# Gathering an expert's two vectors as two transfers instead of one, in a one-core transformer kernel

## The chip, the cores and the metric

The kernel runs on one core of a Trainium2 chip (trn2). The metric is the device time of one execution in microseconds (us), as a median of several runs. A difference of about 0.2% (4.6 us) is the least that counts here.

## What is computed

Two transformer blocks over 256 tokens of width 2048. The first block has a mixer (gated linear attention beside dilated attention) and then a mixture of very many small experts; the second has three mixers, cross attention to a memory of 256 rows, and a last norm. The change lies in the expert part of the first block, which is:

```python
def peer_ffn(xn, w_query, sub_keys, expert_down, expert_up):
    ...
    top_s, top_i = lax.top_k(sc, PEER_TOPK)
    ...
    best_s, best_pos = lax.top_k(cand_s, PEER_TOPK)
    idx = jnp.take_along_axis(cand_i, best_pos, axis=-1)
    gates = jax.nn.softmax(best_s, axis=-1)
    K = PEER_HEADS * PEER_TOPK

    def block(args):
        xb, ib, gb = args
        u = expert_down[ib]
        act = jax.nn.gelu(jnp.einsum('tkd,td->tk', u, xb).astype(f32))
        vv = expert_up[ib]
        return jnp.einsum('tk,tkd->td', (gb * act).astype(vv.dtype), vv)
```

There are 16,384 experts. Each has a down vector and an up vector of 2048 float32 (8 KB each). Each token has 8 heads, and each head picks 16 experts, so each token takes 128 experts: it multiplies its own normed row with the down vector, puts the result through gelu, weighs it with the gate, and adds that multiple of the up vector to its output.

## The kernel before

The kernel is written for the engines one by one, with semaphores. The function `peer` holds the expert stage. The tokens stand in two tiles of 128, one token in each partition. A unit is one head of one tile, 16 units in all (`UNITS`), with 16 experts each (`K`); the counter `d = n * K + j` runs over 256 steps, and a step is one expert for each of 128 tokens.

`slots` is a ring of four slots (`DEPTH = 4`). A slot has two halves of 8 KB in each partition: half 0 for the down vector, half 1 for the up vector. The array `peer_rows` in memory has an expert's down and up vector side by side, 16 KB a row (made in `lay_out`). What each engine does in a step:

- POOL waits until the unit's row numbers are written (`selected`), and until the add of four steps earlier is over (`added`), and then issues one indirect DMA (L1635): 128 rows of 16 KB, 2 MB. It counts up `row_in` of the slot when landed.
- DVE waits for `row_in` and multiplies half 0 with the normed tokens, summed to one number a token (`dotted`, L1727; in the trace CUSTOM_DVE_ANT_0 and the READ_ACCUMULATOR behind it). Text and headings here call this the dot.
- ACT waits for the dot, computes gelu, multiplies with the gate, waits for the add two steps earlier, and scales the identity with the result (L1569, L1570, L1573; `diag_ready`).
- PE waits for `diag_ready` and multiplies this diagonal matrix with half 1 in four matmuls of 512 columns (L1495), which add up in four PSUM banks over a whole tile. This is the add; it counts up `added`. PE has no wait for the gather of its own, since the dot of the same slot lies behind the same landing.

Beside these steps, in the same order of each engine's code: for the first six units PE computes the query of unit n + 2, two of its matmuls a step (L1464), ahead of that step's add; DVE selects the experts of unit n + 1 in pieces ahead of the dots of steps 1 to 6 (`SELECT_AT`), the last of which writes `rows`, the row numbers of the gathers; ACT and DVE compute the gates at steps 8 and 10 (`GATE_AT`). In units 7 to 13 the memory of the second block is loaded (SP), normed, transposed and multiplied with its key and value weights. Ahead of the dot of step 1 of unit 8, DVE waits for the last add of the first tile and adds the four banks to the residual (`take_sums`, L1700), and PE's first add of the second tile waits for that. After the last add the same is done for the second tile, and only then does the second block begin.

SP loads the query weights and the memory's weights in transfers of 1 MB with rows of 8 KB (`load_query`, L1380), on the hardware queue q1. The gathers run on the software queue q0.

The row numbers have two buffers, by the unit's parity.

Of the kernel before, what the change touches and what calls it, by code (L numbers as in the profile page):

```python
# [1382 lines left out]
def peer(k, query_in, keys_in, gain_in, rstd, name="peer"):  # L1383
    nc, ins, B = k.nc, k.ins, k.banks
    UNITS, K, DEPTH = NT * PEER_H, PEER_TOP, 4
# [11 lines left out]
    slots = shaped(k.ring[:, :], DEPTH, 2, D)  # L1397
# [12 lines left out]
    rows = area.take(2, K).bitcast(U32)  # L1410
# [14 lines left out]
    S = lambda n: k.sem(f"{name}_{n}")  # L1425
    query_done, query_out, scored, stored, staged_done = S("query_done"), S("query_out"), S("scored"), S("stored"), S("staged")
    first_query, first_out, first_scored, first_staged = (S(n) for n in ("first_query", "first_out", "first_scored", "first_staged"))
    selected, gated, gates_ready, own, act_own = (S(n) for n in ("selected", "gated", "gates_ready", "own", "act_own"))
    dotted, added, diag_ready, acc_out, gained = (S(n) for n in ("dotted", "added", "diag_ready", "acc_out", "gained"))
    mem_in, mem_squared, mem_meaned, mem_rooted, mem_own, mem_scaled, mem_turned, mem_out = (S(n) for n in (  # L1430
        "mem_in", "mem_squared", "mem_meaned", "mem_rooted", "mem_own", "mem_scaled", "mem_turned", "mem_out"))
    row_in = [S(f"row_in{i}") for i in range(DEPTH)]

    with nc.Block() as block:
        @block.sync
# [13 lines left out]
        def _(pe):  # L1449
# [38 lines left out]
            def add_row(n, j):  # L1488
                d = n * K + j
                first, last = n % PEER_H == 0 and j == 0, n % PEER_H == PEER_H - 1 and j == K - 1  # L1490
                if first and n:
                    pe.wait_ge(acc_out, 4)
                pe.wait_ge(diag_ready, d + 1)
                for c in range(4):
                    m = pe.matmul(B[c][:, :], diag[:, d % 2, :], slots[:, d % DEPTH, 1, c * 512:(c + 1) * 512], start=first, stop=last)  # L1495
                m.then_inc(added, 1)
# [128 lines left out]

        @block.gpsimd
        def _(pool):
            for n in range(UNITS):
                pool.wait_ge(selected, n + 1)
                for j in range(K):  # L1630
                    d = n * K + j
                    if d >= DEPTH:
                        pool.wait_ge(added, d - DEPTH + 1)
                    pool.nop(nofuse=True)
                    pool.indirect_dma_start(slots[:, d % DEPTH, :, :].rearrange("p a b -> p (a b)"), None, ins["peer_rows"],  # L1635
                                            bass.IndirectOffsetOnAxis(ap=rows[:, n % 2, j:j + 1], axis=0)) \
                        .then_inc(row_in[d % DEPTH], 16)

        @block.vector
        def _(dve):  # L1640
# [19 lines left out]
            def select(n, p):  # L1660
                for c in range(2):
                    if n == 0 and c == 0:
                        dve.wait_ge(first_staged, 1)
                    else:
                        dve.wait_ge(staged_done, n + 1)
                    top16(staged[:, p, c, :], top[:, p, c, :], top_i[:, c, :], rest[:, c, :])
                    yield
                dve.tensor_copy(top_f[:, :, :], top_i[:, :, :])
                step(dve.tensor_tensor(cand[:, 0, :, :], top[:, p, 0, :].unsqueeze(2).to_broadcast([P, K, K]),
                                       top[:, p, 1, :].unsqueeze(1).to_broadcast([P, K, K]), ALU.add))  # L1670
                yield
                top16(flat(cand[:, 0, :, :]), best[:, p, :], best_i, flat(cand[:, 1, :, :]))
                yield
                dve.tensor_scalar(low[:, p, :], best[:, p, 0:1], -1.0, None, ALU.mult)
                dve.tensor_scalar(part_i[:, 0, :], best_i, 4, None, ALU.logical_shift_right)
                step(dve.tensor_scalar(part_i[:, 1, :], best_i, 15, None, ALU.bitwise_and))
                step(dve.tensor_copy(part_f[:, :, :], part_i[:, :, :]))
                for c in range(2):
                    m = dve.tensor_tensor(hot[:, c, :, :], part_f[:, c, :].unsqueeze(2).to_broadcast([P, K, K]),
                                          k.c("iota").unsqueeze(1).to_broadcast([P, K, K]), ALU.is_equal)  # L1680
                step(m)
                yield
                for c in range(2):
                    m = dve.tensor_tensor(hot[:, c, :, :], hot[:, c, :, :], top_f[:, c, :].unsqueeze(1).to_broadcast([P, K, K]),
                                          ALU.mult)
                step(m)
                step(dve.tensor_reduce(pair[:, :, :], hot[:, :, :, :], AX.X, ALU.add))
                dve.scalar_tensor_tensor(rows[:, p, :], pair[:, 0, :], float(PEER_K), pair[:, 1, :], ALU.mult, ALU.add) \
                   .then_inc(selected, 1)

# [14 lines left out]
            for n in range(UNITS):  # L1705
                p, t = n % 2, n // PEER_H
                pieces = select(n + 1, 1 - p) if n + 1 < UNITS else iter(())
                for j in range(K):
# [14 lines left out]
                            dve.tensor_scalar(mem[:, m, :], mem[:, m, :], mem_ms[:, m:m + 1], None, ALU.mult).then_inc(mem_scaled, 1)  # L1723
                    d = n * K + j
                    row = slots[:, d % DEPTH, 0, :]
                    dve.wait_ge(row_in[d % DEPTH], 16 * (d // DEPTH + 1))
                    dve.tensor_tensor_reduce(row, row, xn[:, t, :], 1.0, 0.0, ALU.mult, ALU.add, dots[:, p, j:j + 1]) \  # L1727
                       .then_inc(dotted, 1)
            take_sums(1)
# [1181 lines left out]
def lay_out(i):  # L2911
    a = {}
# [40 lines left out]
    a["w_query"] = blocks_of(i["peer_w_query"][0], 2 * PEER_K)  # L2953
    a["sub_keys"] = np.ascontiguousarray(i["peer_sub_keys"][0].transpose(3, 0, 1, 2).reshape(P, 2 * PEER_H, PEER_K))
    a["norm2_row"] = rows(i["norm2_g"])
    a["peer_rows"] = np.concatenate([i["peer_down"][0], i["peer_up"][0]], axis=1)
    parts = {}
    for n, v in (("norm1_g", "norm1_g"), ("norm2_g", "norm2_g"), ("mix_g", "mix_norm_g_2"), ("xa_g", "xa_norm_g_2"),
                 ("mem_g", "mem_norm_g_2")):
# [18 lines left out]
```

## Time and profile before

| | us |
|---|---|
| runs (3): median, lowest, highest | 2311.83, 2311.35, 2314.30 |
| profiled execution, its own time | 2310.28 |
| profiled execution, span from first to last instruction | 2308.5 |
| PE busy | 2056.2 (89%) |
| DVE busy | 1293.5 (56%) |
| ACT busy | 810.2 (35%) |
| POOL busy | 266.9 (12%) |
| software queue q0 (gathers): 36864 packets, 536.89 MB | 54.8% of 16 engines' span |
| hardware queue q1 (all other loads and stores): 53232 packets, 191.63 MB | 25.9% |
| first gather to last add | 470.6 to 1792.0 |

The busy time of an engine is an average over very different parts of the kernel. In the expert stage the DMA engines are the ones to look at: the profile gives for any stretch the mean busy share of the 16 DMA engines and the bytes that they moved. Times of waits are idle time of an engine just before an instruction, put down to what released it. The TensorE clock in the expert stage was granted in full but for short drops (mean 0.98 from 480 to 1784 us).

### The profile page before, as it was taken

The numbers are of one execution on the slowest core, as the hardware profiler recorded it, in microseconds if no ns is written. First come the engines' busy times: TensorE is split into PE (matmuls) and PEld (weight loads), VectorE is DVE, ScalarE is ACT, GpSimd is POOL, SyncE is SP. The second block draws the span as 40 slices with busy tenths as digits, with TensorE's granted clock in tenths as the row PEclk, the third lists the DMA queues.
The fourth block names the chain that finished last, engine by engine and source line by source line (L and its number), as shares of the span: only waits on it lengthen the run. The fifth ranks groups of instructions, "written<-read, shape, count | busy, mean of one in ns | idle before, by whom it ended". The sixth has DMA issues, their size and how long they took to land. (4 is left out here: it accounts for less than half of the span.)

```text
span 2308.5 us, 21761 instructions
## 1 busy us (share of the span) xinstructions
PE 2056.2 (89%) x8141; PEld 1333.0 (58%) x8141; DVE 1293.5 (56%) x2008; ACT 810.2 (35%) x1743; POOL 266.9 (12%) x267
## 2 busy tenths in 40 slices
PE   7999999989988989977777898899877799999997
PEld 6878778854444444422223344444322798999886
DVE  5545655455555556545566555555644766475555
ACT  6445564312222222212222222122122555355453
POOL 0000000011122112122121111211211000000000
PEclk9999999999999999989999999999999899999999
DMA  6545566499999999999999999999998656466662
GB/s 231 165 133 160 163 191 202 185 376 428 428 426 427 428 427 424 428 427 415 428 412 428 428 428 426 427 424 428 409 429 380 210 155 181 125 204 203 183 194 80
DMA packets 90201, 729.90 MB, mean 316 GB/s; under 512 B 10448, under 2 KB 10704, under 8 KB 53104
## 3 DMA queue, kind: packets, MB, share of 16 engines
q0 software_dynamic: 36864, 536.89, 54.8%
q1 hardware_dynamic: 53232, 191.63, 25.9%
q8 instruction: 64, 1.05, 0.2%
q14 instruction: 41, 0.34, 0.0%
HBM read 724.28 MB, written 4.19 MB: 316 GB/s over the span
## 5 line engine op out<-in xcount | busy, mean ns | idle before, releaser
L1495 PE MATMUL bank<-ring,work 128*128 128x512 f32 x2048 | 964.4, 615 | 199.0 <-ACT work L1573 196.2
L1727 DVE CUSTOM_DVE_ANT_0 ring<-ring,mix_t 128x2048 f32<-128x2048 f32 x256 | 586.8, 2292 | 555.4 <-DMA ring<-in_peer_rows_dram,work 553.4
L1495 PEld LDWEIGHTS bank<-ring,work 128*128 128x128 f32 x2048 | 375.6, 193 | 712.5 <-issue 379.2
L490 DVE TENSOR_TENSOR ring_r<-ring,ring_r 128x1024 fp32r<-128x1024 f32 (+2 forms) x300 | 334.5, 1144 | 306.0 <-ACT ring_r L469 305.4
L1635 POOL DMA_INDIRECT ring<-in_peer_rows_dram,work x256 | 262.9, 1027 | 1508.7 <-PE bank L1495 952.9
L523 PE MATMUL bank<-ring_r,mix_r 128*128 128x512 f32 (+1 forms) x1312 | 400.8, 392 | 0.0
L1569 ACT ACTIVATE work<-work 128x1 f32<-128x1 f32 x256 | 51.9, 203 | 959.0 <-DVE work L1727 958.9
L469 ACT ACTIVATE ring_r<-ring 128x1024 fp32r<-128x1024 f32 (+2 forms) x300 | 288.5, 992 | 166.3 <-DMA ring<-in_w_out_dram 50.5
L523 PEld LDWEIGHTS bank<-ring_r,mix_r 128*128 128x128 f32 x1312 | 244.6, 189 | 47.0 <-issue 1.0
L523 PE MATMUL bank<-ring_r,act_r 128*128 128x512 f32 (+1 forms) x608 | 234.6, 386 | 0.0
L520 PE MATMUL bank<-mix_r,ring_r 128*128 128x256 f32 (+1 forms) x1216 | 225.9, 288 | 5.6 <-DVE ring_r L490 5.6
L520 PEld LDWEIGHTS bank<-mix_r,ring_r 128*128 128x128 f32 (+1 forms) x1216 | 190.6, 191 | 7.4 <-DVE ring_r L490 4.1
L520 PE MATMUL bank<-act_r,ring_r 128*128 128x256 f32 (+1 forms) x608 | 173.1, 285 | 0.0
L1464 PEld LDWEIGHTS bank<-act_t,h 128*128 128x128 f32 x544 | 102.9, 190 | 62.8 <-issue 55.0
L1464 PE MATMUL bank<-act_t,h 128*128 128x256 f32 x544 | 137.2, 379 | 0.0
L523 PEld LDWEIGHTS bank<-ring_r,act_r 128*128 128x128 f32 x608 | 114.7, 189 | 22.2
L520 PEld LDWEIGHTS bank<-act_r,ring_r 128*128 128x128 f32 (+1 forms) x608 | 116.1, 191 | 0.0
L1573 ACT ACTIVATE work<-const,work 128x128 f32<-128x128 f32 x256 | 102.8, 401 | 8.4
L523 PE MATMUL bank<-ring_r,h_r 128*128 128x512 f32 x288 | 83.2, 394 | 0.9 <-DVE h_r L2788 0.9
L1570 ACT ACTIVATE work<-work 128x1 f32<-128x1 f32 x256 | 75.3, 294 | 8.3
L523 PEld LDWEIGHTS bank<-ring_r,h_r 128*128 128x128 f32 x288 | 53.8, 188 | 12.7 <-DVE h_r L2788 1.3
L523 PE MATMUL bank<-ring_r,work_r 128*128 128x512 f32 x192 | 59.8, 392 | 0.0
(397 smaller groups left out, 1233.4 us busy)
## 6 DMA issues: line engine op xcount, KB each, us to landing
ring<-in_w_in_dil_dram SPq DMA_DIRECT2D x72, 512.0 KB, 3.6
ring<-in_w_out_dram SPq DMA_DIRECT2D x64, 512.0 KB, 3.6
ring<-in_w_in_mo_dram SPq DMA_DIRECT2D x48, 384.0 KB, 3.4
h<-in_w_query_dram SPq DMA_DIRECT2D x15, 1024.0 KB, 11.4
ring<-in_w_in_gla_dram SPq DMA_DIRECT2D x24, 512.0 KB, 3.6
ring<-in_w_in_ml_oz_dram SPq DMA_DIRECT2D x24, 512.0 KB, 3.7
h<-in_xa_wkv_dram SPq DMA_DIRECT2D x8, 1024.0 KB, 22.4
ring<-in_w_in_lru_dram SPq DMA_DIRECT2D x16, 512.0 KB, 3.6
```

The lines of the kernel that those rows point to most:

```text
L469: act.activation(high(c), raw(c), ACT.Copy).then_inc(k.weights_high, 1)
L490: dve.tensor_tensor(low(c), raw(c), plain(high(c)), ALU.subtract).then_inc(k.weights_low, 1)
L520: m = pe.matmul(bank[0:job.m, 0:T], w[:, q, g * job.m:(g + 1) * job.m], a[:, q, :], start=start, stop=stop)
L523: m = pe.matmul(bank[:, 0:job.cols], a[:, q, g * P:(g + 1) * P], w[:, q, :], start=start, stop=stop)
L1464: m = pe.matmul(bank[:, f * T:(f + 1) * T], a, w, start=kc == 0, stop=kc == KC - 1)
L1495: m = pe.matmul(B[c][:, :], diag[:, d % 2, :], slots[:, d % DEPTH, 1, c * 512:(c + 1) * 512], start=first, stop=last)
L1569: step(act.activation(gelu[:, p, j:j + 1], dots[:, p, j:j + 1], ACT.Gelu_apprx_tanh))
L1570: step(act.activation(coef[:, p, j:j + 1], gelu[:, p, j:j + 1], ACT.Copy, scale=gates[:, p, j:j + 1]))
L1573: act.activation(diag[:, d % 2, :], k.c("ident"), ACT.Copy, scale=coef[:, p, j:j + 1]).then_inc(diag_ready, 1)
L1635: pool.indirect_dma_start(slots[:, d % DEPTH, :, :].rearrange("p a b -> p (a b)"), None, ins["peer_rows"], bass.IndirectOffsetOnAxis(ap=ro ...
L1727: dve.tensor_tensor_reduce(row, row, xn[:, t, :], 1.0, 0.0, ALU.mult, ALU.add, dots[:, p, j:j + 1]) \
```

## The change

The two vectors of an expert come from two arrays, `peer_down` and `peer_up`, with 8 KB a row, and by two indirect DMAs of 1 MB each. Each of them has its own semaphores, `down_in` and `up_in`. POOL asks for the down vectors of step d as soon as the dot of step d - 4 is over (`dotted`), and behind that for the up vectors of step d - 1 as soon as the add of step d - 5 is over (`added`). So the order on the queue is down 0, down 1, up 0, down 2, up 1, and so on. DVE's dot waits for `down_in`. PE's add waits for `up_in` as well, behind `diag_ready`. Since row numbers are now read one step later, DVE waits ahead of writing the row numbers of unit n for the last add of unit n - 2.

```diff
-    row_in = [S(f"row_in{i}") for i in range(DEPTH)]
+    down_in = [S(f"down_in{i}") for i in range(DEPTH)]
+    up_in = [S(f"up_in{i}") for i in range(DEPTH)]
...
                 pe.wait_ge(diag_ready, d + 1)
+                pe.wait_ge(up_in[d % DEPTH], 16 * (d // DEPTH + 1))
...
         @block.gpsimd
         def _(pool):
-            for n in range(UNITS):
-                pool.wait_ge(selected, n + 1)
-                for j in range(K):
-                    d = n * K + j
-                    if d >= DEPTH:
-                        pool.wait_ge(added, d - DEPTH + 1)
-                    pool.nop(nofuse=True)
-                    pool.indirect_dma_start(slots[:, d % DEPTH, :, :].rearrange("p a b -> p (a b)"), None, ins["peer_rows"],
-                                            bass.IndirectOffsetOnAxis(ap=rows[:, n % 2, j:j + 1], axis=0)) \
-                        .then_inc(row_in[d % DEPTH], 16)
+            def gather(d, half, source, landed):
+                n, j = divmod(d, K)
+                pool.nop(nofuse=True)
+                pool.indirect_dma_start(slots[:, d % DEPTH, half, :], None, source,
+                                        bass.IndirectOffsetOnAxis(ap=rows[:, n % 2, j:j + 1], axis=0)).then_inc(landed[d % DEPTH], 16)
+
+            def gather_up(d):
+                if d >= DEPTH:
+                    pool.wait_ge(added, d - DEPTH + 1)
+                gather(d, 1, ins["peer_up"], up_in)
+
+            for d in range(UNITS * K):
+                if d % K == 0:
+                    pool.wait_ge(selected, d // K + 1)
+                if d >= DEPTH:
+                    pool.wait_ge(dotted, d - DEPTH + 1)
+                gather(d, 0, ins["peer_down"], down_in)
+                if d:
+                    gather_up(d - 1)
+            gather_up(UNITS * K - 1)
...
+                if n >= 2:
+
+                    dve.wait_ge(added, (n - 1) * K)
                 dve.scalar_tensor_tensor(rows[:, p, :], pair[:, 0, :], float(PEER_K), pair[:, 1, :], ALU.mult, ALU.add) \
                    .then_inc(selected, 1)
...
-                    dve.wait_ge(row_in[d % DEPTH], 16 * (d // DEPTH + 1))
+                    dve.wait_ge(down_in[d % DEPTH], 16 * (d // DEPTH + 1))
...
-    a["peer_rows"] = np.concatenate([i["peer_down"][0], i["peer_up"][0]], axis=1)
+    a["peer_down"], a["peer_up"] = i["peer_down"][0], i["peer_up"][0]
```

## Rows read from the trace of the kernel before

**Rows 1.** The page's slices: 40 of 57.7 us; DMA share in tenths, then GB/s.

```profile
DMA  6545566499999999999999999999998656466662
GB/s 231 165 133 160 163 191 202 185 376 428 428 426 427 428 427 424 428 427 415 428 412 428 428 428 426 427 424 428 409 429 380 210 155 181 125 204 203 183 194 80
```

**Rows 2.** Waits, 480 to 1750: us in total, times, the longest.

```profile
POOL ring L1635 <- PE bank L1495: 932.7, 224, 20.2
...
DVE ring L1727 <- DMA ring<-in_peer_rows_dram,work: 532.7, 226, 5.1
```

**Rows 3.** Stretches: length, busy us (instructions) by engine, PE clock, DMA share, GB/s.

```profile
500.00:505.00 5.00, 5.00 (x15) 2.50 (x15) 4.58 (x11) 0.90 (x3) 3.56 (x2) 1.00 0.85 311
1060.00:1070.00 10.00, 7.40 (x16) 2.88 (x16) 5.38 (x9) 2.29 (x8) 3.54 (x3) 1.00 0.87 346
1155.00:1175.00 20.00, 16.21 (x35) 6.11 (x34) 14.61 (x33) 6.37 (x15) 6.62 (x4) 0.98 0.93 382
1610.00:1630.00 20.00, 18.25 (x49) 8.79 (x50) 9.20 (x8) 3.81 (x13) 5.58 (x5) 1.00 0.94 387
...
1690.00:1780.00 90.00, 68.05 (x148) 26.60 (x149) 41.40 (x36) 16.17 (x54) 16.38 (x18) 1.00 1.01 428
480.00:1784.00 1304.00, 1105.39 (x2768) 505.85 (x2767) 720.47 (x1090) 301.94 (x885) 258.97 (x252) 0.98 1.00 424
```

**Rows 4.** DMA queues, 1100 to 1150: packets, MB, their time over 16 engines' stretch.

```profile
q0 software_dynamic: 1477, 21.35, 100.4%
```

**Rows 5.** DMA queues, 459 to 462: loads with rows of 8 KB alone.

```profile
DMA packets 174, 1.29 MB, mean 431 GB/s; under 512 B 16, under 2 KB 16, under 8 KB 16
...
q1 hardware_dynamic: 174, 1.29, 102.1%
```

**Rows 6.** DMA queues, 730 to 745: gathers beside loads with rows of 8 KB.

```profile
q0 software_dynamic: 312, 4.51, 71.0%
q1 hardware_dynamic: 256, 1.84, 29.3%
```

**Rows 7.** The gathers' line, L1635: the last row of its view.

```profile
DMA to landing us min/median/max: 8.8/11.7/25.0
```

**Rows 8.** Timeline near the stage's end: start, us, engine, line, what, idle before.

```profile
1760.44 2.29 DVE L1727 CUSTOM_DVE_ANT_0 ring<-ring,mix_t 128x2048 f32<-128x2048 f32 x1 [2.61 <-DMA ring<-in_peer_rows_dram,work]
...
1763.79 3.70 PE L1495 MATMUL bank<-ring,work 128*128 128x512 f32 x8 [1.20 <-ACT work L1573]
1765.34 2.29 DVE L1727 CUSTOM_DVE_ANT_0 ring<-ring,mix_t 128x2048 f32<-128x2048 f32 x1 [2.60 <-DMA ring<-in_peer_rows_dram,work]
...
1768.27 0.94 POOL L1635 DMA_INDIRECT ring<-in_peer_rows_dram,work  x1 [3.97 <-PE bank L1495]
...
1784.90 2.29 DVE L1727 CUSTOM_DVE_ANT_0 ring<-ring,mix_t 128x2048 f32<-128x2048 f32 x1 [2.58 <-DMA ring<-in_peer_rows_dram,work]
...
1788.26 3.70 PE L1495 MATMUL bank<-ring,work 128*128 128x512 f32 x8 [1.18 <-ACT work L1573]
```

**Rows 9.** Timeline, 1055 to 1065: an add and the gather that waits for it.

```profile
1055.53 3.70 PE L1495 MATMUL bank<-ring,work 128*128 128x512 f32 x8 [1.20 <-ACT work L1573]
...
1062.69 2.40 POOL L1635 DMA_INDIRECT ring<-in_peer_rows_dram,work  x1 [6.65 <-issue]
```

**Rows 10.** Timeline at the boundary of the two tiles.

```profile
1148.79 2.48 DVE L1700 TENSOR_TENSOR x_res<-bank,x_res 128x512 f32<-128x512 f32 x4
...
1153.08 2.29 DVE L1727 CUSTOM_DVE_ANT_0 ring<-ring,mix_t 128x2048 f32<-128x2048 f32 x1
...
1157.49 2.82 POOL L1635 DMA_INDIRECT ring<-in_peer_rows_dram,work  x1 [7.05 <-PE bank L1495]
```

**Rows 11.** Timeline at the stage's start: the first dot and the fifth gather.

```profile
483.97 2.28 DVE L1727 CUSTOM_DVE_ANT_0 ring<-ring,mix_t 128x2048 f32<-128x2048 f32 x1
...
495.61 0.93 POOL L1635 DMA_INDIRECT ring<-in_peer_rows_dram,work  x1 [20.20 <-PE bank L1495]
```

**Rows 12.** Timeline: the query matmuls of one step.

```profile
507.56 1.03 PE L1464 MATMUL bank<-act_t,h 128*128 128x256 f32 x4
```

## What is expected, worked out before the changed kernel was run

> **What bounds the kernel now.** I read the page's slices first, then the waits, then the stage in stretches, then single DMA queues, then the timeline. The slices show a stage of some 1300 us (slices 9 to 31 of 57.7 us) in which the DMA engines stand at 9 tenths and carry 409 to 429 GB/s in all but the first and the last slice [rows 1]. That is the expert stage: 256 gathers of 2 MB, 536.9 MB of the 729.9 MB of the whole kernel. The waits of that stretch say the same from the engines' side: DVE stands 532.7 us for the gathered rows, and POOL stands 932.7 us for PE to give a slot back [rows 2]. POOL's number is the larger one, but it is no bottleneck as long as transfers asked for earlier still keep the DMA engines busy. So the question for each edit is what it does to the bytes per microsecond, not what it does to a wait.
>
> The stretches answer how full the DMA is [rows 3]: 428 GB/s at share 1.01 where nothing disturbs (1690 to 1780 us), 424 GB/s over the stage from 480 to 1784 us. At 428 GB/s a gather of 2,097,152 bytes takes 4.90 us, which is the distance of two dots in the timeline (1760.44 to 1765.34) [rows 8]. The missing part is 1304 x (1 - 424/428) = 12.2 us. Four stretches hold most of it: 5 x (1 - 311/428) = 1.4, 10 x (1 - 346/428) = 1.9, 20 x (1 - 382/428) = 2.1, 20 x (1 - 387/428) = 1.9, together 7.4 us, and in these the DMA share is below 1: the engines have run dry. The other 4.8 us lie spread in stretches with a full share and I count them as not to be had.
>
> **Why it runs dry.** Four slots of 2 MB. A slot is asked for again when its add is over: from the start of dot 1760.44 the add runs 1763.79 to 1767.49 and POOL starts the new gather at 1768.27, 7.8 us after the data came [rows 8]. The landing takes 11.7 us in the median, 8.8 at the least [rows 7]; 7.8 + 11.7 = 19.5 is four times 4.9. An undisturbed gather could come 11.7 - 8.8 = 2.9 us sooner than it does, so 2.9 us is about how late POOL may be before the engines go empty. It is later in the four stretches: at 1062.69 the gather starts 3.5 us after PE ended its add (1055.53 + 3.70) and takes 2.40 instead of 0.94 [rows 9]; after the first tile's sums (DVE 2.48 us, which PE waits for) POOL starts at 1157.49 after 7.05 us idle and takes 2.82 [rows 10]; at the start the fifth gather goes out only at 495.61, 11.6 us after the first dot starts [rows 11].
>
> **The change part by part.**
>
> Depth of the queue (gain). The down half of a slot is now free after its dot, and the up half after its add; 8 transfers of 1 MB (2.45 us each) stand in the place of 4 of 2 MB. When a down vector lands, seven others of 1 MB are asked for or on their way: 7 x 2.45 = 17.1 us. Its half is asked for again after the dot (2.29) and POOL's step, about 3.3 us: 13.8 us in hand. For an up half: add 3.70 and POOL's 0.8, 4.5 us, 12.6 us in hand. The same count for before is 3 x 4.90 - 7.8 = 6.9. So the tighter of the two gains 12.6 - 6.9 = 5.7 us on top of the 2.9 us, 8.6 us. The stops above are 3 to 5 us and are covered. At the start the fifth down vector can go out at the end of the first dot (486.3) and not at 495.61. I count the whole of the 7.4 us as gained. The bounds are 0 (the stops stay) and 12.2 us (all of the shortfall).
>
> The boundary of the tiles is the place that becomes harder. DVE, ahead of the second dot of the second tile, waits for the last add of the first, and now dots run ahead of adds: an up vector lands 7.3 us (three transfers) after its down vector. With T the landing of down vector 128, up vector 127 lands at T + 2.45, its add ends at T + 6.2, the sums (2.48) at T + 8.7, and with the piece of expert selection behind them (1151.27 to the dot at 1153.08, 1.8 us) [rows 10] dot 129 starts at T + 10.5 and not at T + 4.9. Behind it on POOL stand down vector 133 and all that follows, 5.6 us late. That is inside the 8.6 us, though not by much; I cost it at nothing, and at some 2 us if the cover is smaller.
>
> The end (gain). Before, the chain behind the last byte is dot 1784.90, ACT, add 1788.26 to 1791.96: 7.1 us [rows 8]. Now the order of landing is down 255, up 254, up 255. If the last byte comes at the same 1784.90, up 254 is there at 1782.45, its add ends at 1786.15, and the last add ends at 1786.15 + 3.70 = 1789.85. That is 2.1 us less; the last dot and its ACT steps lie under the two up vectors.
>
> Rows of 8 KB for rows of 16 KB (cost). The bytes stay the same, the packets of the gathers double: 128 rows of 8 KB and 16 small packets in each of 512 transfers. What a 16 KB packet takes: 1477 packets of 21.35 MB are 1303 rows, 1.004 x 50 us x 16 engines = 803 us, 0.6164 us each with its share of the small ones [rows 4]. What an 8 KB packet takes is not shown for a gather, but for the 1 MB loads of the query weights. Alone on the engines: 1.29 MB are 158 rows, 1.021 x 3 us x 16 = 49.0 us, 0.3102 us each, at 431 GB/s in that short stretch [rows 5]. Beside gathers: 1.84 MB are 225 rows, 0.293 x 15 x 16 = 70.3 us, 0.3125 us each, where a 16 KB packet of the same stretch takes 0.710 x 240 / 275 = 0.6196 [rows 6]. Two halves against one whole, times the 8 rows that an engine has of a gather and 256 gathers (2048): (0.6204 - 0.6164) x 2048 = 8.2 us from the stretch with one queue, (0.6250 - 0.6196) x 2048 = 11.1 us from the mixed one, and 0 if one reads the 431 GB/s. The worst pair of these numbers, 0.6250 against 0.6164, gives 17.6 us, and one more small packet for each engine and gather (some 9 ns by difference of these rows, an estimate) 20 us. I take 8.2, since there, as in the expert stage, one queue has the engines nearly to itself.
>
> POOL. 512 gathers in place of 256. Each costs 0.94 us, and at most the 0.8 us from an add's end to POOL's start (1767.49 to 1768.27) [rows 8] for what stands between two, so at most 3.4 us of each 4.9. A long one (2.82) [rows 10] makes that 5.3 once, which the 8.6 us in hand cover. POOL stays faster than the DMA. POOL works in order: down vector d waits for dot d - 4, and behind it up vector d - 1 for add d - 5. That add ends 3.7 us after its up vector's landing, 1.1 us before dot d - 3 ends, for which the next command waits, so in the steady state neither holds up the other.
>
> PE's wait for the up vector, and DVE's wait for earlier adds. PE's wait stands ahead of the four matmuls of an add, behind the query matmuls of that step; these run while the vector is on its way. Queued behind it is the next step's query. PE has 3.70 busy of 4.90, with a query step of 1.03 [rows 12] it is 4.73: still under. DVE's added wait, ahead of the write of the gather's row numbers, is for adds of a whole unit (16 experts, 78 us) earlier and costs nothing.
>
> **The sum.** The profiled execution: 2310.3 us, of which the span is 2308.5; 2310.3 - 7.4 - 2.1 + 8.2 = 2309.0. The median of the runs is 2311.8, 1.5 above the profiled one, so the forecast is 2310.5.
>
> **The rivals.**
> 1. Small packets cost nothing. For it: the 431 GB/s of the stretch with 8 KB rows alone. Against it: in both stretches two 8 KB packets last longer than one of 16 KB. The time: 2311.8 - 7.4 - 2.1 = 2302.3, and 2297.5 if the whole 12.2 us come back. Chance 0.27 for this side.
> 2. Small packets cost more than the deeper queue gives. The place is each DMA engine, 4096 more rows of its own; the price is 17.6 to 20 us, and the time 2311.8 - 9.5 + 20 = 2322.3, slower. It decides from (9.5 + 4.6) / 2048 = 7 ns for each 16 KB on. For it: the 0.3125 us beside gathers, and that a gather's rows are scattered while the weights' are not. Against it: the 4 to 5 ns that like-for-like rows give. Chance 0.21.
> 3. The queue gets no deeper in effect, since POOL works in order and a late add holds back down vectors too. The stops stay, the cost of the rows is paid: 2311.8 - 2.1 + 8.2 = 2317.9. Against it: the 1.1 us above and 8.6 us in hand. Chance 0.05.
> 4. A transfer's own fixed time. Each transfer would be paid for with a part that does not overlap. The trace: landing takes 11.7 us and yet one gather is done each 4.90 us [rows 7, 8], so such a part is under other transfers, and 1 MB loads alone reached 431 GB/s [rows 5]. If 1 MB ran at 80% of the rate of 428, the stage's 537 MB would take 314 us more, 2626. Chance 0.01. The Trainium skill, "DMA: Bandwidth & Descriptors", section "Bandwidth", gives 341 GB/s for a transfer of 1 MB and 425 for 16 MB, and asks for 1 MiB or more; by its two figures the change would be much slower, and by that rule the trace disagrees, since its figures are for transfers one by one.
>
> **How the numbers follow.** The forecast's own case (within 4.6 us, 0.2%, about the least that a measurement of this kernel tells from no change) has 0.46, from 2307 to 2316. Faster by over 0.2%: 0.27. Within: 0.46. Slower: 0.27, from rivals 2, 3 and 4. The range holds rival 1 down to 2300 and rival 2 up to 2325; the bare bounds, 2297.5 and 2331.8 (cost 20 and no gain), lie outside with what is left.
>
> **What the profile after would show.** Gathers: 512, and 73,728 packets on the software queue. If the queue's depth is right, the four stretches have a DMA share of 1 and no slice of the stage under 425 GB/s but for the ends. If the price of the rows is right, two dots are 4.93 us apart in the undisturbed part (4.90 for rival 1, 4.97 for rival 2), and the mean of an 8 KB packet is 0.310 us. DVE's waits for rows should shrink little, since the bytes bound it; PE should now wait for the DMA (up vectors) instead of ACT. Landing should become longer (some 17 us), which is no loss. The last add should end 5 us behind the last dot's place in time. The prediction is wrong if the gathers' rate falls below 424 GB/s in undisturbed stretches, or if new dry stretches appear at the tiles' boundary.

## The result and the profile after

| | before | after |
|---|---|---|
| runs: median, lowest, highest (us) | 2311.59, 2310.40, 2314.30 (4 runs) | 2326.27, 2325.08, 2327.23 (4 runs) |
| profiled execution, its own time and span (us) | 2310.28, 2308.5 | 2327.14, 2325.4 |
| software queue q0: packets, MB | 36864, 536.89 | 73728, 536.90 |
| POOL busy (us) | 266.9 | 547.1 |

The ratio is 1.0062, with a 95% interval of 1.0044 to 1.0079: 14.7 us slower by the medians. The forecast was 2310.5 with a range of 2300 to 2325, so the result lies 1.3 us above it, on the side of rival 2.

The page of the changed kernel: its slices of 58.1 us, the gathers' queue, and the costliest groups of the stage (busy us, mean ns of one, idle before and what ended it).

```profile
DMA  6545566499999999999999999999998656466662
GB/s 230 163 136 161 159 194 208 175 391 421 421 421 421 421 421 422 421 421 421 422 421 421 421 422 421 422 421 419 422 421 370 203 146 186 124 204 200 186 194 80
...
q0 software_dynamic: 73728, 536.90, 55.5%
...
L1497 PE MATMUL bank<-ring,work 128*128 128x512 f32 x2048 | 955.2, 610 | 223.3 <-DMA ring<-in_peer_up_dram,work 197.6
...
L1633 POOL DMA_INDIRECT ring<-in_peer_up_dram,work x256 | 286.8, 1120 | 637.4 <-PE bank L1497 618.6
```

Against [rows 1] two things have changed. The dips (415, 412, 409) are gone: the stage's rate is level. And the level is 421 and not 428. PE now waits for the up vectors, as intended. The same stretches as in [rows 3], of the changed kernel (length, busy us and instructions of PE, PEld, DVE, ACT, POOL, PE clock, DMA share, GB/s):

```profile
500.00:505.00 5.00, 5.00 (x17) 2.88 (x17) 4.13 (x11) 1.30 (x4) 3.36 (x3) 1.00 1.01 421
1060.00:1070.00 10.00, 7.38 (x17) 2.88 (x16) 4.60 (x4) 2.10 (x7) 3.96 (x4) 1.00 1.01 419
1155.00:1175.00 20.00, 16.31 (x33) 6.36 (x33) 16.78 (x37) 2.70 (x9) 9.99 (x8) 0.91 1.01 417
1610.00:1630.00 20.00, 18.31 (x49) 8.79 (x48) 9.20 (x8) 3.60 (x12) 7.93 (x9) 1.00 1.01 420
1690.00:1780.00 90.00, 66.59 (x146) 26.06 (x145) 41.40 (x36) 16.58 (x55) 35.72 (x37) 1.00 1.01 421
480.00:1784.00 1304.00, 1083.91 (x2745) 501.63 (x2743) 716.66 (x1086) 300.20 (x877) 534.67 (x504) 0.98 1.01 421
```

The four dry stretches (shares 0.85 to 0.94 before) all stand at 1.01. So the queue does not run dry there any more, and what is lost is lost all along the stage. The timeline of the changed kernel shows it in the dots, and what follows the last of them (start, us, engine, line, what, idle before):

```profile
1741.82 2.29 DVE L1742 CUSTOM_DVE_ANT_0 ring<-ring,mix_t 128x2048 f32<-128x2048 f32 x1 [2.67 <-DMA ring<-in_peer_down_dram,work]
...
1786.54 2.29 DVE L1742 CUSTOM_DVE_ANT_0 ring<-ring,mix_t 128x2048 f32<-128x2048 f32 x1 [2.67 <-DMA ring<-in_peer_down_dram,work]
...
1796.43 2.29 DVE L1742 CUSTOM_DVE_ANT_0 ring<-ring,mix_t 128x2048 f32<-128x2048 f32 x1 [2.63 <-DMA ring<-in_peer_down_dram,work]
...
1799.00 7.10 PE L1497 MATMUL bank<-ring,work 128*128 128x512 f32 x16 [1.25 <-DMA ring<-in_peer_up_dram,work]
1806.14 2.48 DVE L1715 TENSOR_TENSOR x_res<-bank,x_res 128x512 f32<-128x512 f32 x4 [7.41 <-PE bank L1497]
```

Between the first two rows lie nine experts: 44.72 / 9 = 4.969 us each. The same count of before gives (1784.90 - 1760.44) / 5 = 4.892 [rows 8]. The difference is 0.077 us an expert, and times 256 it is 19.7 us. The first gather starts at 471.2 (470.6 before), and the last dot at 1796.43 (1784.90 before): 11.5 us later, 11.0 without the later start. The sums follow at 1806.14; before, they followed the end of the last add at 1791.96 [rows 8] at once. That is 14.2 us later. The span is 16.9 us longer; the other 2.7 us lie behind the stage, in these two executions, and the medians of the runs, 14.7 us apart, do not call for them.

### The profile page after: what moved, and what is told of

It reads as the page before. It is cut to its first block and busy times, and to the rows that moved or that the text cites. A ratio compares the mean times of both kernels' runs of the same rounds, so it can differ in the third digit from the quotient of the medians.

```text
span 2325.4 us, 22538 instructions
## 1 busy us (share of the span) xinstructions
PE 2047.4 (88%) x8141; PEld 1334.4 (57%) x8141; DVE 1294.8 (56%) x2008; ACT 811.5 (35%) x1743; POOL 547.1 (24%) x523
## 3 DMA queue, kind: packets, MB, share of 16 engines
q0 software_dynamic: 73728, 536.90, 55.5%
## 5 line engine op out<-in xcount | busy, mean ns | idle before, releaser
L1633 POOL DMA_INDIRECT ring<-in_peer_up_dram,work x256 | 286.8, 1120 | 637.4 <-PE bank L1497 618.6
L1633 POOL DMA_INDIRECT ring<-in_peer_down_dram,work x256 | 256.3, 1001 | 606.6 <-DVE work L1703 468.6
```

Of the source, the lines that this page charges most:

```text
L1633: pool.indirect_dma_start(slots[:, d % DEPTH, half, :], None, source, bass.IndirectOffsetOnAxis(ap=rows[:, n % 2, j:j + 1], axis=0)).then_ ...
```

## The experiments

The kernel before was run beside each, and the ratios are against it. Its medians lie between 2311.3 and 2312.8.

**Is it the two arrays, or the size of a row?** The changed kernel, reading both halves from the old array with 16 KB a row, in 8 KB pieces:

```diff
+            both = ins["peer_rows"].rearrange("n (a b) -> (n a) b", a=2)
...
-                pool.indirect_dma_start(slots[:, d % DEPTH, half, :], None, source,
-                                        bass.IndirectOffsetOnAxis(ap=rows[:, n % 2, j:j + 1], axis=0)).then_inc(landed[d % DEPTH], 16)
+                pool.indirect_dma_start(slots[:, d % DEPTH, half, :], None, both,
+                                        bass.IndirectOffsetOnAxis(ap=rows[:, n % 2, j:j + 1], axis=0), half * D).then_inc(landed[d % DEPTH], 16)
...
+                step(dve.tensor_scalar(pair[:, :, :], pair[:, :, :], 2.0, None, ALU.mult))
```

> The changed kernel, but both transfers read halves of 8 KB out of the one array of before (its rows of 16 KB lie side by side; row numbers doubled, up vectors at an offset of half a row). Theory 'rows': what costs is that an engine moves 16 rows of 8 KB for an expert in place of 8 of 16 KB. Then two dots stay 4.97 us apart in the undisturbed stretch and the time stays at that of the changed kernel, 2326 us (within 2). Rival 'two arrays': what costs is that the vectors lie in two arrays. Then the distance goes back to 4.90 us and the time to 2302 to 2308, since the dry stretches are gone.

Measured: 2325.61 us, ratio 1.0066 (1.0050 to 1.0083). Its dots are 4.98 us apart:

```profile
1746.79 2.29 DVE L1745 CUSTOM_DVE_ANT_0 ring<-ring,mix_t 128x2048 f32<-128x2048 f32 x1 [2.67 <-DMA ring<-in_peer_rows_dram,work]
1751.77 2.29 DVE L1745 CUSTOM_DVE_ANT_0 ring<-ring,mix_t 128x2048 f32<-128x2048 f32 x1 [2.68 <-DMA ring<-in_peer_rows_dram,work]
```

So where the halves lie in memory makes no difference that can be seen. The loss comes with asking for them in two pieces.

**Does the price grow with the number of pieces?** The changed kernel with the up vector split once more, in two arrays of 4 KB a row:

```diff
-                gather(d, 1, ins["peer_up"], up_in)
+                gather(d, 1, ins["peer_up_0"], up_in, 0)
+                gather(d, 1, ins["peer_up_1"], up2_in, 1)
```

> The changed kernel with the up vector in two arrays of half vectors, so three transfers for an expert: one of 128 rows of 8 KB, two of 128 rows of 4 KB. An engine now has 24 rows and 3 small packets for an expert; 8 and 1 before, 16 and 2 in the changed kernel. Theory 'rows': the same step once more, 0.077 us for an expert: dots 5.05 us apart, 2326 + 20 = 2346 us. Rival 'order': the loss of the change comes from the order of the two transfers and the waits behind it, which stay: 4.97 us and 2326. If POOL's commands were what bounds, three of them (3 x 1.24 = 3.7 us and the long ones) would give dry stretches with a DMA share under 1.

Measured: 2342.39 us, ratio 1.0139 (1.0122 to 1.0156), another 16 us where theory 'rows' had 20. In the timeline the dots are 5.04 us apart, and the slices have fallen to 415, two of them to 404 and 408:

```profile
GB/s 229 162 139 161 162 196 217 156 411 415 415 415 416 415 416 413 416 416 415 416 404 408 414 415 416 416 415 416 415 416 415 207 147 192 124 198 203 183 197 81
...
q0 software_dynamic: 110592, 536.92, 56.5%
...
1747.83 2.29 DVE L1746 CUSTOM_DVE_ANT_0 ring<-ring,mix_t 128x2048 f32<-128x2048 f32 x1 [2.75 <-DMA ring<-in_peer_down_dram,work]
1752.87 2.29 DVE L1746 CUSTOM_DVE_ANT_0 ring<-ring,mix_t 128x2048 f32<-128x2048 f32 x1 [2.74 <-DMA ring<-in_peer_down_dram,work]
```

An engine moves for each expert 8 rows and a small packet (before), 16 and 2 (after), 24 and 3 (here). The steps are 0.077 and 5.04 - 4.97 = 0.07 us, for 8 more rows and one more small packet each time: 9 to 10 ns for each row more, its part of the small packet included, whether rows of 16 KB are halved or rows of 8 KB. Row and small packet came together in every kernel, so these runs do not divide the price between them.

**Is the new order worth anything?** The changed transfers, with the old asking: both halves behind the add, down d and then up d.

```diff
-                    pool.wait_ge(dotted, d - DEPTH + 1)
+                    pool.wait_ge(added, d - DEPTH + 1)
                 gather(d, 0, ins["peer_down"], down_in)
-                if d:
-                    gather_up(d - 1)
-            gather_up(UNITS * K - 1)
+                gather(d, 1, ins["peer_up"], up_in)
```

> The changed kernel's two transfers and four slots, but both halves asked for behind the add, in the order down d, up d. The run with three slots and this order took 2395 us, more than any count had given, since the count left out what a landing needs beside its moving: 6.9 us at the least for 1 MB, 4.4 more than the 2.5 of moving. In hand then: three slots 9.9 - 5.7 - 4.4 = -0.2, four slots 14.9 - 5.7 - 4.4 = 4.8 us. Theory 'rows' (with the corrected count): no loss beside the changed kernel, distance 4.97 us, 2326 us within 3. Rival 'the new order is worth something by itself, and late asking is what costs': some 20 us or more above, 2345.

Measured: 2325.17 us, ratio 1.0058 (1.0042 to 1.0074), the same as the changed kernel. The dots are 4.97 us apart, and one slice of the stage dips to 405. So neither the order nor the early asking is worth anything that can be seen here, and the cost of the pieces is most of what the change does to the time.

**What would a deeper queue be worth without smaller rows?** The kernel before with a fifth slot. Its memory is that of the residual, so this kernel adds the sums to the normed tokens and computes another function.

```diff
-    UNITS, K, DEPTH = NT * PEER_H, PEER_TOP, 4
+    UNITS, K, DEPTH = NT * PEER_H, PEER_TOP, 5
...
-    slots = shaped(k.ring[:, :], DEPTH, 2, D)
+    ring4 = shaped(k.ring[:, :], 4, 2, D)
+    slot = lambda d: ring4[:, d % DEPTH, :, :] if d % DEPTH < 4 else k.x3
```

> The kernel before (one transfer of 2 MB with rows of 16 KB) with five slots in place of four. The fifth lies where the residual x stood, so the residual is not kept: the expert sums are added to the normed tokens instead, and tile 0 is copied over at the stage's end beside the last sums. That gives depth alone, without small rows. In hand: 4 x 4.90 - 7.8 - 3.9 (the least landing 8.8 less 4.9 of moving) = 7.9 us, against 3.0 with four slots. Theory 'depth gives the dry stretches back': distance 4.90 us, no slice of the stage under 425 GB/s, 2312 - 7.4 = 2304 to 2306 us. Rival 'slowest engine': the mean rate rises, but one of the 16 DMA engines has more to do and sets the landing of each gather; the time stays at 2309 to 2312 and the stage ends with a tail in which the DMA share is 0.1 or less.

Measured: 2310.03 us (11 runs), ratio 0.9989 (0.9979 to 0.9998). Its slices, two dots, the sums, and the last microseconds of the gathers:

```profile
GB/s 232 164 130 163 164 185 207 181 387 428 427 427 428 428 428 427 428 425 428 429 427 429 428 427 428 428 425 416 429 428 338 214 152 180 125 204 203 183 194 80
...
1752.53 2.29 DVE L1730 CUSTOM_DVE_ANT_0 x_res<-x_res,mix_t 128x2048 f32<-128x2048 f32 x1 [2.60 <-DMA x_res<-in_peer_rows_dram,work]
1757.42 2.29 DVE L1730 CUSTOM_DVE_ANT_0 ring<-ring,mix_t 128x2048 f32<-128x2048 f32 x1 [2.59 <-DMA ring<-in_peer_rows_dram,work]
...
1788.93 2.48 DVE L1703 TENSOR_TENSOR x_res<-bank,mix_t 128x512 f32<-128x512 f32 x4 [4.79 <-PE bank L1496]
...
1774.00:1776.00 2.00, 0.80 (x3) 0.31 (x3) 0.41 (x2) 0.90 (x3) 0.00 (x0) 1.00 0.81 344
1776.00:1778.00 2.00, 2.00 (x6) 0.94 (x5) 1.00 (x1) 0.00 (x0) 0.00 (x0) 1.00 0.15 66
1778.00:1780.00 2.00, 1.16 (x3) 0.19 (x1) 1.29 (x2) 0.61 (x3) 0.00 (x0) 1.00 0.06 25
1780.00:1782.00 2.00, 1.66 (x4) 0.87 (x5) 0.16 (x1) 0.29 (x1) 0.00 (x0) 1.00 0.04 16
```

The dips are gone but for one slice (416), and the kernel gains only 3.0 us at the sums (1791.96 to 1788.93) and 2.5 us by the ratio, where the prediction put 7.4 on the dips. The last four rows say why: most of the engines have moved all their data by 1776, and then a share of 0.06, one engine of sixteen, moves on at 25 GB/s until about 1781.4. A gather counts as landed when its last engine is done, so the mean rate is not what sets the dots; the engine that is last is.

The dots of the kernel before say the same. These are the two on either side of the third and of the fourth dry stretch of [rows 3]:

```profile
1161.34 2.29 DVE L1727 CUSTOM_DVE_ANT_0 ring<-ring,mix_t 128x2048 f32<-128x2048 f32 x1 [1.41 <-DMA ring<-in_peer_rows_dram,work]
1168.00 2.29 DVE L1727 CUSTOM_DVE_ANT_0 ring<-ring,mix_t 128x2048 f32<-128x2048 f32 x1 [1.90 <-DMA ring<-in_peer_rows_dram,work]
...
1621.16 2.29 DVE L1727 CUSTOM_DVE_ANT_0 ring<-ring,mix_t 128x2048 f32<-128x2048 f32 x1 [2.57 <-DMA ring<-in_peer_rows_dram,work]
1626.49 2.29 DVE L1727 CUSTOM_DVE_ANT_0 ring<-ring,mix_t 128x2048 f32<-128x2048 f32 x1 [3.04 <-DMA ring<-in_peer_rows_dram,work]
```

The four stretches lengthened one distance of two dots each: to 5.52 us (the dot at 510.04), 5.48 (1072.30), 6.66 and 5.33, together 3.4 us more than four times 4.89. With five slots the same four distances are 4.88, 5.01, 4.89 and 4.89. So these stretches held back the dots by about 3 us, and not by the 7.4 us that the mean rate had lost. The trace also keeps the landing of each of the sixteen parts of a gather. In the last stretch the first part of one gather came 7.5 us behind the first part of the one before it, and the last part 5.3 us behind the last: the engine that was ahead lost 2.6 us, and the one that was last 0.4 us.

The Trainium skill, "DMA: Bandwidth & Descriptors", section "Why a DMA increments its semaphore by 16 and not by 1", says that the up to 16 engines of a transfer finish independently and that only the full count means that all data landed. The trace agrees: the last dot, at 1781.84, comes when the single engine stops.

**Do dry stretches cost anything at all?** The changed kernel with three slots in place of four.

```diff
-    UNITS, K, DEPTH = NT * PEER_H, PEER_TOP, 4
+    UNITS, K, DEPTH = NT * PEER_H, PEER_TOP, 3
```

> The changed kernel with three slots in place of four. By the count of the prediction the tighter half has 5 x 2.49 - 4.5 = 7.9 us in hand, near the 6.9 of the kernel before, against 12.6 with four. Theory 'depth gave back what the dry stretches cost': some of the dry stretches come back, 2326 + 3 to 8, so 2329 to 2334. Rival 'slowest engine': the end of the gathers is set by those of the 16 DMA engines that lag (in the changed kernel a small part of them works some 6 us longer than the rest at the stage's end), and a deeper queue only lets the others run ahead. Then fewer slots cost nothing: 2324 to 2327, and the tail at the end is shorter.

Measured: 2327.67 us, ratio 1.0078 (1.0061 to 1.0094); the intervals of this and of the changed kernel overlap. Its slices and the end of its gathers, beside the end of those of the changed kernel:

```profile
GB/s 230 163 136 162 160 195 208 173 392 415 419 421 421 421 421 411 422 421 422 422 407 421 419 422 421 422 421 419 422 421 410 202 150 184 125 204 200 186 194 80
...
1796.00:1800.00 4.00, 2.76 (x8) 1.00 (x7) 2.30 (x2) 0.34 (x2) 0.00 (x0) 1.00 0.88 326
1800.00:1804.00 4.00, 4.00 (x10) 1.83 (x11) 0.00 (x0) 2.04 (x4) 0.00 (x0) 1.00 0.03 14
```

```profile
1792.00:1796.00 4.00, 2.73 (x7) 0.99 (x6) 1.80 (x2) 0.90 (x3) 0.00 (x0) 1.00 0.74 309
1796.00:1800.00 4.00, 2.75 (x8) 1.00 (x7) 2.30 (x2) 1.15 (x4) 0.00 (x0) 1.00 0.10 43
1800.00:1804.00 4.00, 4.00 (x11) 1.83 (x10) 0.00 (x0) 1.23 (x2) 0.00 (x0) 1.00 0.01 4
```

Dry stretches have come back (415, 411, 407) and the time has not moved. Most of the engines finish some 4 us later than with four slots (share 0.88 in place of 0.10 from 1796 to 1800), and the last one finishes within 1 us of where it did (its last part lands at 1802.2, and at 1801.3 with four slots). A dry stretch takes time mostly from engines that were ahead.

**How much reserve is there at each depth?** Two kernels, the changed one with three slots and the old asking, and the kernel before with three slots. The edits are those already shown.

> Three slots as in the run with depth 3, and both halves of a slot are asked for together, behind the add of the step that used it, as before the change (down d, then up d). In hand: 2 x 4.97 - 4.5 = 5.4 us, less than the 6.9 of the kernel before. Undisturbed distance of dots 4.97 by 'rows'. Theory 'depth': more dry time than the kernel before had (7.4 us in the four stretches), so 2326 + 9 to 15: 2335 to 2341. Rival 'slowest engine': 2326 to 2330. This is also the changed kernel without its new order, so if the order itself were at fault, the distance would fall under 4.97.

> The kernel before with three slots of 2 MB. In hand by the corrected count: 2 x 4.90 - 7.8 - 3.9 = -1.9 us, so the landing time and not the rate of the DMA engines would bound it: a slot turns once in 7.8 + 8.8 = 16.6 us, dots 5.5 us apart, 256 x 0.63 = 160 us more, 2470 us. If the count is wrong and only the rate matters: 2312 to 2330 us.

Measured: 2395.0 us, ratio 1.0376 (1.0324 to 1.0428), and 2593.81 us, ratio 1.1218 (1.1197 to 1.1239, two runs of it). A count of one slot's turn says where the loss begins. A slot is asked for again 7.8 us after its data came [rows 8], and the shortest landing follows, 8.8 us for 2 MB [rows 7]. This turn, at least 16.6 us, has to fit into as many periods as there are slots. Before: 4 x 4.89 = 19.6, 3 us to spare. Before with three slots: 14.7, too little. Changed, three slots, old asking, with its own shortest landing: 7.8 + 6.8 = 14.6 against 3 x 4.97 = 14.9, nothing to spare. The last rows of the landing view of the kernel before with three slots, and of the changed one with three slots and the old asking:

```profile
DMA to landing us min/median/max: 7.9/9.8/16.1
```

```profile
DMA to landing us min/median/max: 6.8/8.9/18.3
```

The count does not say how much is lost. The forecast of 2470 divided the 16.6 us by three slots, 5.5 us an expert or 160 us in all; 281 were measured. A shortest landing is a floor: with the median landing of this kernel an expert takes (7.8 + 9.8) / 3 = 5.87 us, and 256 x (5.87 - 4.89) = 250 us. Its adds were also slower, which the forecast had not: the granted clock from 480 to 2060 us was 0.91, where it had been 0.98 in the stage before, and its matmuls of the adds were busy for 1062.2 us in place of 964.4. How the rest divides, and why the kernel with the old asking loses 69 us with nothing to spare, these runs do not show.

**Which engine lags?** The kernel with five slots, and in every step instructions on ScalarE that do nothing. At first 20 and 40 empty instructions were written; the profile shows no more instructions than without (21761 in all, 23 packets on the instruction queue q14 from 500 to 1780), so nothing shows that they were in the program that ran.

```diff
+                for _ in range(20):
+                    act.nop(nofuse=True)
```

> The five-slot kernel with 20 instructions more on ACT behind the diagonal of each step, which do nothing; 5120 in the stage. In the five-slot kernel a DMA share of 0.06, one engine of 16, is left at the stage's end for some 4 us, and 21 packets of the queue for instructions (16 KB each) ran between 500 and 1780. Theory 'the lagging engine is the one that also loads instructions': 5120 x 64 bytes, as 1.05 MB for some 16,000 instructions of the engines suggest, are some 20 packets more; at 0.61 us each on one engine 12 us, though only 0.06% of the bytes; 2310 + 10 to 14, so 2320 to 2324, and a longer tail. Rival 'one engine is slower by itself': the time stays within 3 us of 2310, with the 20 packets more. A third, that ACT is stopped while it waits for its instructions: then dry stretches, and the tail does not grow.

> The same with 40 of them in each step. Theory 'instructions on one engine': the step from none to 20 once more, 2330 to 2338 us, in proportion to the packets on the instruction queue. Rival: within 3 us of 2310. ACT has some 4 us idle in a step and 40 such instructions should take 1 to 2.5 us of them, so the chain from dot to add is not longer.

Measured: 2308.75 us (10 runs), ratio 0.9988 (0.9978 to 0.9997), and 2310.04 us (10 runs), ratio 0.9994 (0.9985 to 1.0004). They say nothing on the question, but repeat the kernel with five slots twice: its gain is 1 to 3 us. Then waits on counts that are already reached took their place; of these the profile has 5120 more instructions, 20 a step:

```diff
+                for _ in range(20):
+                    act.wait_ge(gained, 1)
+                    act.wait_ge(gained, 2)
```

> The kernel before with five slots for the 16 KB rows, as in the other five-slot kernels (the first residual is left out: the sums are added to the normed tokens, so the output is another function), plus 40 waits on already met counts in every step on ScalarE, behind the move to the diagonal. They are instructions that ScalarE has to load, 320 KB more of them over the stage, which is 20 packets of 16 KB on the instruction queue q8 (about 41 in place of 21 between 500 and 1780 us). Question: is the one DMA engine that still moves data when the other fifteen are done (share 0.06, 4 to 6 us at the stage's end) the one that also loads the instructions? Theory A, it is: 20 more packets of about 0.61 us each on one of the sixteen engines make it 12 us later, so 2310 becomes 2318 to 2324 and the stretch at a share of 0.06 grows by up to 12 us, while the slices stay near 427 GB/s. Theory B, one engine is slower by itself and the instruction packets go elsewhere or are spread: within 3 us of 2310, the same tail. Theory C, ScalarE itself stands still while instructions are loaded and the diagonals come late: the dots start late, VectorE waits for ScalarE in the waits, and the time rises with no longer tail.

Measured: 2332.56 us, ratio 1.0094 (1.0075 to 1.0113), 22.5 us more than the kernel with five slots. Of this kernel: the instruction queue from 500 to 1780 (packets, MB, share); the same queue in the 2.5 us from 1749.5, as the only such packet there; the dots around it; and the end of the gathers.

```profile
q14 instruction: 61, 0.50, 0.1%
...
q14 instruction: 1, 0.01, 0.8%
...
1739.31 2.29 DVE L1733 CUSTOM_DVE_ANT_0 ring<-ring,mix_t 128x2048 f32<-128x2048 f32 x1 [2.60 <-DMA ring<-in_peer_rows_dram,work]
1744.19 2.29 DVE L1733 CUSTOM_DVE_ANT_0 ring<-ring,mix_t 128x2048 f32<-128x2048 f32 x1 [2.59 <-DMA ring<-in_peer_rows_dram,work]
1749.09 2.29 DVE L1733 CUSTOM_DVE_ANT_0 x_res<-x_res,mix_t 128x2048 f32<-128x2048 f32 x1 [2.60 <-DMA x_res<-in_peer_rows_dram,work]
1754.66 2.29 DVE L1733 CUSTOM_DVE_ANT_0 ring<-ring,mix_t 128x2048 f32<-128x2048 f32 x1 [3.26 <-DMA ring<-in_peer_rows_dram,work]
1759.55 2.29 DVE L1733 CUSTOM_DVE_ANT_0 ring<-ring,mix_t 128x2048 f32<-128x2048 f32 x1 [2.59 <-DMA ring<-in_peer_rows_dram,work]
...
1798.00:1800.00 2.00, 1.75 (x4) 0.87 (x5) 0.32 (x1) 0.20 (x1) 0.00 (x0) 1.00 0.06 25
1800.00:1802.00 2.00, 1.95 (x5) 0.57 (x3) 1.98 (x2) 0.00 (x0) 0.00 (x0) 1.00 0.06 25
1802.00:1804.00 2.00, 0.89 (x2) 0.49 (x3) 0.00 (x0) 0.90 (x3) 0.00 (x0) 1.00 0.06 25
```

Theory A holds, though not on the queue that it named: the added packets are 38 of 8 KB on q14, not 20 of 16 KB on q8 (21 there, as before). The dots stand 4.90 us apart, but the one behind the instruction packet comes after 5.57: DVE waits 3.26 instead of 2.59 us, for a gather and for nothing else. The last dot moved from 1781.84 to 1804.63, which is 22.8 / 38 = 0.60 us for a packet more; at this single dot it is 0.67. The stretch in which a single engine moves data has grown from some 4 to over 6 us, and not by all of the 22.8, because the other fifteen can't run further ahead than the slots allow. So in this kernel the engine that carries ScalarE's instructions is the one that all gathers wait for. Theory C falls: what came late were the gathers, and ScalarE began 0.20 us behind each dot's result as before.

Without the added waits it is the same in small. In the kernel with five slots, the dots around one of its own packets on q14, and that packet in the 3 us from 1518:

```profile
1515.72 2.29 DVE L1730 CUSTOM_DVE_ANT_0 ring<-ring,mix_t 128x2048 f32<-128x2048 f32 x1 [2.57 <-DMA ring<-in_peer_rows_dram,work]
1521.57 2.29 DVE L1730 CUSTOM_DVE_ANT_0 ring<-ring,mix_t 128x2048 f32<-128x2048 f32 x1 [3.21 <-DMA ring<-in_peer_rows_dram,work]
...
q14 instruction: 1, 0.01, 0.7%
```

Seven of its 23 packets on q14 are followed by such a delay, of 0.95 to 1.03 us at the landing of the gather, and most of the others by none. At such packets the last part of a gather falls back behind the fifteenth: 1.0 us before the packet at 1073.9 and 2.0 behind it, 2.0 before the one at 1169.1 and 2.9 behind it, with no change in between. So theory B, an engine that is slower by itself, is not needed to explain why one engine is behind. Whose instructions these seven carry the trace does not say; that they are ScalarE's is argued from the run with the waits.

The packets on q8 are not on that engine: one of 16 KB runs at 1741.3 in the kernel with the waits, and the dots at 1739.31, 1744.19 and 1749.09 keep their distance. It stays open why an added packet costs 0.60 to 0.67 us and one of the seven some 0.95, where a loaded row of the same size took 0.31 us [rows 5].

## Why the prediction was wrong, step by step

**Price of the rows: 8.2 us predicted, 19.7 measured.** This is the step that failed most. A loaded row of 8 KB, 0.3102 us by its records in 3 us of the trace, stood for a gathered one and was set against the records of gathered rows of 16 KB, 0.6164 us. The traces now have both as gathers, over the same 90 us from 1690, before and after:

```profile
q0 software_dynamic: 2644, 38.54, 100.6%
```

```profile
q0 software_dynamic: 5198, 37.88, 101.2%
```

Without the small packets these are 2352 and 4624 rows, in 90 x 16 = 1440 us of engine time. A row of 16 KB takes 1.006 x 1440 / 2352 = 0.6159 us, as it had been read; a gathered row of 8 KB takes 1.012 x 1440 / 4624 = 0.3152 and not 0.3102. But the difference of such records is no price either: it would be (0.6303 - 0.6159) x 2048 = 29 us. Shares above 1 mean that records overlap, and they overlap more with the smaller rows (1.012 against 1.006). What counts is the period of the experts over the eight rows of an engine: 4.892 / 8 = 0.6115 us before and 4.969 / 8 = 0.6211 for two halves after, and 0.0096 x 2048 = 19.7 us. That twice 0.3102 comes close to 0.6211 is chance. Rival 2 had the price (17.6 to 20), and in its remark that gathers and loads may differ it had the weak place; 0.21 was too little for it.

**Depth: 7.4 us predicted, about 3 measured (by the kernel with five slots).** The stretches ran dry for the reason given and filled up as forecast, and the mean rate became level. But the mean rate over sixteen engines was taken for the pace of the stage. The four stretches held back the dots by 3.4 us and not by 7.4; the kernel with five slots has full stretches and gains 2.5 to 3.0 us; the changed kernel with three slots has dry ones and loses 1.4 us, within its noise. The step left out is that a landing waits for the engine that is last, which catches up while the others stand.

**The end: 2.1 us predicted, 2.3 measured.** The last part of the last up vector lands at 1801.3, and the last add ends at 1806.1: 4.8 us in place of 7.1. Right, and by the way described: the two last adds run as one block of 7.10 us.

**POOL, PE's wait, DVE's added wait, the order: nothing predicted, nothing seen.** POOL's busy time doubled to 547.1 us of the span (24%) without a dry stretch. The changed order is worth nothing either way, by the kernel with the old asking. The boundary of the tiles stayed covered (share 1.01 from 1155 to 1175).

**The sum again.** 2310.5 + (19.7 - 8.2) + (7.4 - 3.0) - (2.3 - 2.1) = 2326.2, against 2326.27 measured. The terms were read from the traces after the result, so this says that nothing large is left over, and is no second proof. The changed kernel has 27 packets on the instruction queue q14 in the stage, and the one before 23; the four more are no term of the sum, since in the changed kernel too seven packets are followed by a delay of 0.90 to 0.97 us and of the others only one outside the loads by any, of 0.2 us.

**The other rivals.** Rival 1 falls by the level of 421 GB/s. Rival 3 falls by the shares of 1.01. Rival 4 falls as a size: transfers of 1 MB, overlapped, run at 421 GB/s. The Trainium skill's table ("DMA: Bandwidth & Descriptors", section "Bandwidth") rises with the size of a transfer, from 341 GB/s at 1 MB to 425 at 16 MB. The runs agree in the sign, since fewer and larger pieces are faster here (428, 421, 415 GB/s with 1, 2, 3 pieces an expert), and not in the size: the figure of 341 GB/s does not hold with several transfers in flight.

## What to carry to other kernels

Where DMA bounds a stage, take what a packet costs from the period of the work (bytes or rows over time) and not from the durations of its records, once the share reads above 1, and do not let a load stand for a gather. A dip of the mean DMA rate is not all to be gained: look at how far it held back the work that waits for the transfers (here the distance of two dots), and at the last microseconds of the stage. If the share falls to one engine's part before the end, that engine sets the pace. A deeper queue that is bought with smaller rows is a bad trade once the turn of a slot (use, asking, shortest landing) already fits into its periods: here the depth gave 3 us and the rows took 20.

## What the runs showed of the hardware

- Asking for the same bytes in smaller gathered rows cost 9 to 10 ns for each row more on its engine, small packets included, from 16 to 8 KB and again where half of the bytes went from 8 to 4 KB: 428, 421 and 415 GB/s.
- ScalarE's instructions are loaded through one of the sixteen DMA engines that move the kernel's data. Each packet of 8 KB more delays the stream by 0.60 us on average, seen at a single dot as 5.57 in place of 4.90 us. Straight-line code of that engine is thus paid for in a stage bound by DMA: 38 packets more made it 22.8 us longer.
- Dry stretches that took 7.4 us from the mean rate of sixteen engines held back the gathers by 3.4 us, since they took most from engines that were ahead (in one of them 2.6 us, and 0.4 from the engine that was last).
- A gather of 2 MB took at least 8.8 us from issue to landing with four slots (7.9 with three), while its bytes take 4.9 at the rate of the stage. With three slots the rate from 480 to 1784 us was 351 GB/s, and 424 with four.
